# RWKV inverses as full-array products, and outputs' products with a common stationary merged

## The reference, cut to what matters

```
def step(state, inp):
    r_t, w_t, k_t, v_t, kk_t, a_t = inp
    sa = jnp.einsum('bhvk,bhk->bhv', state, -kk_t)
    state = (state * w_t[:, :, None, :]
             + sa[..., None] * (kk_t * a_t)[:, :, None, :]
             + v_t[..., None] * k_t[:, :, None, :])
    return state, jnp.einsum('bhvk,bhk->bhv', state, r_t)
```

## Time and profile before

| | us |
|---|---|
| median of 3 runs | 2262.66 |
| lowest and highest | 2260.02, 2272.73 |
| profiled execution, its own time | 2271.0 |
| its span in the trace | 2269.2 |
| inverses, 1423.8 to 1484.9 | 61.1 |
| outputs, 1485.6 to 1513.2 | 27.6 |

### The profile page before, as it was taken

One profiled execution on the slowest core, in us unless ns is written; L12 is line 12 of the kernel. 1 busy time (PEld: TensorE's weight loads), 2 busy tenths in 40 slices (PEclk: granted clock), 3 DMA queues, 4 the chain that ended last, 5 costly groups with the idle time before them and its releaser, 6 DMA issues.

```text
span 2269.2 us, 33265 instructions
## 1 busy us (share of the span) xinstructions
PE 2169.4 (96%) x14214; PEld 1782.5 (79%) x14214; DVE 1408.1 (62%) x1456; ACT 1030.6 (45%) x1155; POOL 80.5 (4%) x138
## 2 busy tenths in 40 slices
PE   6999899999999899999999999889999999999999
PEld 4777777688787777778788897777888888887887
DVE  5767744689775744499765655466556675635664
ACT  4344322467545422377644545335445444535443
POOL 2040000000000000000000000000000000020000
PEclk9998899999999899999999998999999999999999
DMA  9863879999660858999555550006555556433553
GB/s 346 329 224 110 292 252 371 366 336 367 207 241 7 275 205 307 331 344 368 186 186 188 167 182 1 4 11 215 186 186 166 195 172 204 147 95 120 195 186 112
DMA packets 267314, 475.62 MB, mean 210 GB/s; under 512 B 9424, under 2 KB 151824, under 8 KB 262944
## 3 DMA queue, kind: packets, MB, share of 16 engines
q1 hardware_dynamic: 256128, 431.81, 54.8%
q0 software_dynamic: 11040, 41.70, 5.5%
HBM read 471.33 MB, written 2.14 MB: 209 GB/s over the span
## 4 chain that ended last, share of the span: by engine, by line
PE 85%; DVE 7%; ACT 4%; DMA 3%; issue 2%; SPq 0%; ACTq 0%; DVEq 0%
PE psum L1069 14%; PE psum L1071 7%; PE psum L1086 3%; PE psum L1088 3%; PE psum L1087 3%; PE psum L1037 3%; PE psum L1038 3%; PE psum L1039 3%; PE psum L1406 3%; PE psum L1361 2%; PE psum L1362 2%; PE psum L1363 2%; PE psum L1518 2%; PE psum L1520 2%; PE psum L1519 2%; DVE w_lo L2798 2%
## 5 line engine op out<-in xcount | busy, mean ns | idle before, releaser
L2798 DVE TENSOR_TENSOR w_lo<-ring,w_hi 128x2048 fp32r<-128x2048 f32 x267 | 609.9, 2289 | 290.8 <-ACT w_hi L2149 284.8
L2149 ACT ACTIVATE w_hi<-ring 128x2048 fp32r<-128x2048 f32 x267 | 510.8, 1915 | 363.9 <-PE psum L1088 119.8
L1069 PE MATMUL psum<-h_both,w_hi 128*128 128x512 f32 x1408 | 499.7, 399 | 1.7 <-DVE h_both L3492 1.3
L1071 PE MATMUL psum<-h_both,w_lo 128*128 128x256 f32 x1408 | 395.3, 281 | 0.0
L1069 PEld LDWEIGHTS psum<-h_both,w_hi 128*128 128x128 f32 x1408 | 264.5, 188 | 68.4 <-issue 1.7
L1071 PEld LDWEIGHTS psum<-h_both,w_lo 128*128 128x128 f32 x1408 | 265.9, 189 | 1.4
L2798 DVE TENSOR_TENSOR w_lo<-pool,w_hi 128x2048 fp32r<-128x2048 f32 x70 | 160.4, 2291 | 107.5 <-ACT w_hi L2149 107.1
L2149 ACT ACTIVATE w_hi<-pool 128x2048 fp32r<-128x2048 f32 x70 | 134.1, 1916 | 163.9 <-DMA pool<-in_exp_w_up 59.2
L2171 ACT ACTIVATE pool<-psum 128x512 f32<-128x512 f32 x88 | 52.6, 598 | 261.5 <-PE psum L1071 261.5
L1037 PE MATMUL psum<-w_hi,h_both 128*128 128x512 f32 (+1 forms) x352 | 141.8, 403 | 6.6 <-DVE w_lo L2798 4.4
L1361 PE MATMUL psum<-h_both,w_hi 128*128 128x256 f32 x480 | 139.1, 290 | 0.6 <-DVE w_lo L2798 0.6
(11 more groups left out here) (476 smaller groups left out, 3813.2 us busy)
## 6 DMA issues: line engine op xcount, KB each, us to landing
ring<-in_ffn_pre_w_in SPq DMA_DIRECT2D x44, 1024.0 KB, 5.1
ring<-in_ffn_post_w_in SPq DMA_DIRECT2D x44, 1024.0 KB, 5.1
pool<-in_exp_w_up SPq DMA_DIRECT2D x40, 1024.0 KB, 7.9
ring<-in_exp_w_gate SPq DMA_DIRECT2D x36, 1024.0 KB, 7.6
ring<-in_exp_w_down SPq DMA_DIRECT2D x30, 1024.0 KB, 7.6
ring<-in_ada_w SPq DMA_DIRECT2D x24, 1024.0 KB, 7.1
ring<-in_ffn_pre_w_out SPq DMA_DIRECT2D x22, 1024.0 KB, 4.9
ring<-in_ffn_post_w_out SPq DMA_DIRECT2D x22, 1024.0 KB, 4.9
```

Of the source, the lines that this page charges most:

```text
L1069: pe.matmul(o.rearrange("p (s n) -> p s n", s=2), wh[:, k, fs], h_both[:, :, k, :], start=k == 0, stop=False, skip_group_check=True)
L1071: m = pe.matmul(o[:, 0:T], wl[:, k, fs], h_hi[:, k, :], start=False, stop=k == KD - 1, skip_group_check=True)
L2149: act.activation(w_hi[:, (s["split"] + r) % 3, :], piece(s["pieces"][r]), ACT.Copy)\
L2798: dve.tensor_tensor(w_lo[:, slot, :], piece(s["pieces"][r]), w_hi[:, slot, :].bitcast(F32), ALU.subtract).then_inc(sem("w_lo"), 1)
```

## The change

L and M are now stored as 128x128 matrices, of which the blocks that would mix two chunks hold zeros. GpSimd writes the zeros once, before the inverses (four memsets); ScalarE then copies L in four pieces for a group where it copied two, each of 64 partitions, into the other blocks, and VectorE masks M in four pieces where it had two. One product with a 128x128 stationary then serves both chunks: X = L T and M v take 4 products for each s in place of 8. In the outputs two products that share a stationary are issued as one with 128 moving columns (`both` makes an address of two strips): the inverse with kk and U, and `neg_g` with b and `out_m`. `neg_g` and `neg_h` move to columns that held L.

```diff
--- before.py
+++ after.py
@@ -354,6 +354,11 @@
         def bank(b, n=1):
             return psum[:, b, :] if n == 1 else psum[:, b:b + n, :].rearrange("p b n -> p (b n)")
 
+        def both(first, second):
+
+            return bass.AP(tensor=first.tensor, offset=first.offset,
+                           ap=[first.ap[0], [second.offset - first.offset, 2], *first.ap[1:]])
+
         def view(off, *dims):
             n = int(np.prod(dims))
             v = pool[:, off:off + n]
@@ -531,13 +536,14 @@
         gate = view(HT, NT, 768)
 
         kk_tok = xn[:, :, 0:768]
-        t_lt = [[view(PROJ + 3072 + 512 * r + 256 * s_, 4, CHUNK) for s_ in range(2)] for r in range(2)]
-        t_t = [view(PROJ + 4096 + 256 * s_, 4, CHUNK) for s_ in range(2)]
-        t_x = [view(PROJ + 4608 + 256 * s_, 4, CHUNK) for s_ in range(2)]
-        t_m = [view(PROJ + 5120 + 256 * s_, 4, CHUNK) for s_ in range(2)]
+        t_lt = [[view(PROJ + 3072 + 1024 * r + 512 * s_, 4, P) for s_ in range(2)] for r in range(2)]
+        t_t = [view(PROJ + 5120 + 256 * s_, 4, CHUNK) for s_ in range(2)]
+        t_x = [view(PROJ + 5632 + 256 * s_, 4, CHUNK) for s_ in range(2)]
+        t_m = [view(PROJ + 6144 + 512 * s_, 4, P) for s_ in range(2)]
+        t_lt_all, t_m_all = view(PROJ + 3072, 16, P), view(PROJ + 6144, 8, P)
         turn = pool[:, ROWS + 1536:ROWS + 3840].rearrange("p (w c n) -> p w c n", w=2, c=3)
-        neg_g = [view(PROJ + 5632 + 512 * r, NT, P) for r in range(2)]
-        neg_h = [view(PROJ + 5888 + 512 * r, NT, P) for r in range(2)]
+        neg_g = [view(PROJ + 3072 + 512 * r, NT, P) for r in range(2)]
+        neg_h = [view(PROJ + 3328 + 512 * r, NT, P) for r in range(2)]
         out_m = [
             pool[:, WORK + 4608 + 512 * r:WORK + 5120 + 512 * r].rearrange("p (e w t n) -> p e w t n", e=2, w=2, t=NT)
             for r in range(2)]
@@ -870,6 +876,11 @@
             pl.dma_start(view(ROWS + 3072, 1024), scratch_mem[0]).then_inc(sem("mem_in"), 16)
             pl.wait_ge(sem("norm_T"), 8 * (NORMS.index("n_mix0") + 1))
             pl.dma_start(rw_reset, a["c_reset"]).then_inc(sem("route_in"), 16)
+            pl.wait_ge(sem("rw_bonus_ps"), 1)
+            pl.memset(t_lt_all[0:64, :, 0:64], 0.0)
+            pl.memset(t_lt_all[64:P, :, 64:P], 0.0)
+            pl.memset(t_m_all[0:64, :, 64:P], 0.0)
+            pl.memset(t_m_all[64:P, :, 0:64], 0.0).then_inc(sem("rw_lt"), 1)
             pl.wait_ge(sem("x_new"), 7)
             pl.dma_start(view(ROWS + 3072, 1024), scratch_mem[1]).then_inc(sem("mem_in"), 16)
             pl.wait_ge(sem("x_new"), 8)
@@ -1782,16 +1793,13 @@
                                     m.then_inc(sem("rw_tt_ps"), 1)
                     if l < 5:
                         if l == 0:
-                            pe.wait_ge(sem("rw_lt"), 2 * g + 2)
+                            pe.wait_ge(sem("rw_lt"), 4 * g + 5)
                         for s in range(2):
                             pe.wait_ge(sem("rw_t"), 10 * g + 2 * l + s + 1)
                             for m4 in range(4):
-                                for q in range(2):
-                                    m = pe.matmul(bank(s)[halves[q], 64 * m4:64 * m4 + 64], t_lt[g % 2][s][halves[1 - q], m4, :],
-                                                  t_t[s][halves[1 - q], m4, :], start=True, stop=True)
-                                    m_last[q] = m
-                            for m in m_last:
-                                m.then_inc(sem("rw_x_ps"), 1)
+                                m = pe.matmul(bank(s)[:, 64 * m4:64 * m4 + 64], t_lt[g % 2][s][:, m4, :], t_t[s][:, m4, :],
+                                              start=True, stop=True)
+                            m.then_inc(sem("rw_x_ps"), 2)
                     if l == 0:
                         chunk_products(g, (6, 7), Fk, W[3])
                         for m in m_last:
@@ -1801,13 +1809,9 @@
                         for s in range(2):
                             i = 2 * g + s
                             for m4 in range(4):
-                                for hq in halves:
-                                    v = v_tok[hq, m4 % 2, P * i + 64 * (m4 // 2):P * i + 64 * (m4 // 2) + 64]
-                                    m = pe.matmul(bank(6 + s)[hq, 64 * m4:64 * m4 + 64], t_m[s][hq, m4, :], v,
-                                                  start=True, stop=True)
-                                    m_last[hq.start // 64] = m
-                            for m in m_last:
-                                m.then_inc(sem("rw_u_ps"), 1)
+                                v = v_tok[:, m4 % 2, P * i + 64 * (m4 // 2):P * i + 64 * (m4 // 2) + 64]
+                                m = pe.matmul(bank(6 + s)[:, 64 * m4:64 * m4 + 64], t_m[s][:, m4, :], v, start=True, stop=True)
+                            m.then_inc(sem("rw_u_ps"), 2)
                     if l == 4 and g < 2:
                         pe.wait_ge(sem("rw_u"), 2 * g + 2)
                         later(g + 1)
@@ -1843,11 +1847,10 @@
                         pe.wait_ge(sem("rw_gh"), 1)
                     for m4 in range(4):
                         t, o = m4 % 2, 128 * i + 64 * (m4 // 2)
-                        for w, right in enumerate((kk_tok, U)):
-                            for hq in halves:
-                                m = pe.matmul(bank(3)[hq, P * m4 + 64 * w:P * m4 + 64 * w + 64], TT[hq, i, m4, :],
-                                              right[hq, t, o:o + 64], start=True, stop=True)
-                                m_last[hq.start // 64] = m
+                        for hq in halves:
+                            m = pe.matmul(bank(3)[hq, P * m4:P * m4 + P].rearrange("p (w n) -> p w n", w=2), TT[hq, i, m4, :],
+                                          both(kk_tok[hq, t, o:o + 64], U[hq, t, o:o + 64]), start=True, stop=True)
+                            m_last[hq.start // 64] = m
                     for m in m_last:
                         m.then_inc(sem("rw_gh_ps"), 1)
                 if i >= 1:
@@ -1860,14 +1863,18 @@
                     begun -= {(6, 0), (6, 1), (7, 0), (7, 1)}
                     quarters = [(e, q) for e in range(2) for q in range(2)]
                     for t in range(NT):
-                        for e, q in quarters:
-                            m_last[q] = pe.matmul(bank(6 + q)[halves[e], 256 + 64 * t:320 + 64 * t], neg_g[r][halves[q], t, halves[e]],
-                                                  out_m[r][halves[q], e, 0, t, :], start=first(6 + q, e), stop=True,
-                                                  skip_group_check=True)
                         ahead = [(e, q, slice(P * j + 64 * e, P * j + 64 * e + 64)) for e, q in quarters if 2 * t + q < 3]
                         for e, q, cols in ahead:
-                            pe.matmul(bank(6 + q)[halves[e], 64 * t:64 * t + 64], neg_g[r][halves[q], t, halves[e]],
-                                      b_tok[halves[q], t, cols], start=False, stop=True, skip_group_check=True)
+                            m_last[q] = pe.matmul(both(bank(6 + q)[halves[e], 64 * t:64 * t + 64],
+                                                       bank(6 + q)[halves[e], 256 + 64 * t:320 + 64 * t]),
+                                                  neg_g[r][halves[q], t, halves[e]],
+                                                  both(b_tok[halves[q], t, cols], out_m[r][halves[q], e, 0, t, :]),
+                                                  start=first(6 + q, e), stop=True, skip_group_check=True)
+                        if t == 1:
+                            for e in range(2):
+                                m_last[1] = pe.matmul(bank(7)[halves[e], 320:384], neg_g[r][halves[1], t, halves[e]],
+                                                      out_m[r][halves[1], e, 0, t, :], start=False, stop=True,
+                                                      skip_group_check=True)
                         for e, q, cols in ahead:
                             pe.matmul(bank(6 + q)[halves[e], P + 64 * t:P + 64 * t + 64], b_tok[halves[q], t, cols],
                                       neg_h[r][halves[q], t, halves[e]], start=False, stop=False, skip_group_check=True)
@@ -2490,8 +2497,10 @@
 
                 act.wait_ge(sem("rw_l_ps"), 4 * g + 2)
                 for s in range(2):
-                    act.activation(t_lt[g % 2][s].rearrange("p (e t) n -> p e (t n)", e=2),
-                                   psum[:, 6:8, P * s:P * s + P], ACT.Copy).then_inc(sem("rw_lt"), 1)
+                    dst = t_lt[g % 2][s].rearrange("p (e t) n -> p e t n", e=2)
+                    src = psum[:, 6:8, P * s:P * s + P].rearrange("p e (t n) -> p e t n", t=NT)
+                    for q in range(2):
+                        act.activation(dst[halves[1 - q], :, :, halves[q]], src[halves[1 - q]], ACT.Copy).then_inc(sem("rw_lt"), 1)
 
             later(0)
             for g in range(3):
@@ -3410,10 +3419,13 @@
             def tiles(v):
```

(11 more changed lines are left out.)

## The result

The changed kernel takes 2272.98 us (median of 19 runs, 2267.36 to 2279.52), the kernel before 2261.69 (19 runs beside it, 2256.85 to 2272.73). The ratio is 1.0048, with a 95% interval of 1.0039 to 1.0057. That is 10.9 us slower (8.8 to 12.9), where the predicted 2272.0 stood for +9.3 us. All ratios here leave out one run that was much slower at a mean granted clock of 0.65 (3103.26 us, of the kernel with M v on quarters).

A forecast was written before the change was run, and what follows sets the result against it. Two close limits on TensorE: instruction supply in 16 KB blocks, at best one in 3.8 us, and the products' time. 17.6 - 5.9 - 2.4 - 0 = +9.3 us on 2262.7 gives 2272.0; eight in ten from 2256 to 2282.

The forecast's parts named there:

- X and M v, +17.6: Inverses: half as many full-array records, each nearly four times as costly; 5.9 us a group, three groups +17.6.
- The full drain: Changes between full array and quarters: draining TensorE, 0.22 us at 30 changes, would add 3 us to the sum.
- What was costed at nothing: VectorE's four masks of M, ScalarE's two more copies of L and POOL's memsets: all hidden, 0 us.
- The refund, -5.9: Inverses: 288 fewer records end all seven instruction pauses, 4.7 us of idle and 0.16 each hidden.
- Outputs, -2.4: Outputs: merged products -0.3, pauses before 1499 gone -1.9, a last bit near 1511 -0.2.
- The third pause: Outputs, L1848 at 1501.6: removing its 0.6 us gives nothing, as TensorE then waits for VectorE's mask.
- half the clock behind the longer wait: Outputs: the wait for VectorE might cool the clock and cost more than now (0.94 granted); a sign of being wrong.
- The free full array: Rival: X's full-array records run at 0.058, as fast as quarter pairs; 2254 to 2256 us; chance 0.13.
- the refund that does not come: Rival: pauses not due to the instruction count, so the 8 us stay; +17.3, 2280 us; chance 0.15.
- the hidden X: Rival: VectorE's and ScalarE's round trip sets the levels, X grows beside it; 2257 to 2259 us; chance 0.10.

The follow-up runs named there:

- The shifted streams: Kernel before with 32, then 16, small products put ahead of the chunk products; inverses 59.57 us and 60.99 us.
- the added waits: Four long-met waits after each m4 of X: in the kernel before ratio 1.0057, inverses 71.92 us; in the changed kernel 1.0065, 73.83 us.
- the run with half of X: Kernel before with only m4 = 0 and 1 of the X products, the other half left out; inverses 54.72 us.
- the run with the split moved: Kernel before with merged outputs, one weight split moved from round 3 to 5 on ScalarE and behind the rounds on VectorE; ratio 0.9982, outputs 21.31 us.
- Outputs alone: Kernel before with only the outputs' products merged, L and M left in quarters; ratio 0.9991, outputs 23.43 us.

## Why the prediction was right

The change measured +10.9 us (8.8 to 12.9) for the forecast of +9.3. That the time itself, 2272.98, lies within 1 us of 2272.0 is luck in part, since the kernel before took 1 us less beside it than the 2262.66 the forecast started from. Two of the sums are 0.1 to 0.2 off: three groups of 5.9 are 17.7, and 4.7 and seven times 0.16 are 5.8, so the whole comes to +9.5 with its own terms.

**X and M v, +17.6: right.** The table above gives 5.9 a group. The 0.16 for the first and 0.112 for the other records came out at 1.72 us for 15 of them, 0.115; X to T at a plain level at 1.93 for the 1.90 taken; level 2 at 3.72 for 3.7. Inside the group parts were off and cancel: level 0 cost 1.00 in place of 1.4, level 4 cost 1.17 in place of 0.8, and 0.31 of level 1's 0.93 are VectorE's masks, which the prediction had at nothing. Without them X and M v are 5.6 a group, 16.9 in all, and the masks 0.9; that the two together hit 17.6 is luck. The change back to quarters, 0.07 before the end of the last full record in the earlier trace rows, was 0.07 here too (1.72 + 0.275 - 1.93), and the comparison with M v on quarters gives it as 0.09 a change. The full drain of the Trainium skill (TensorEngine Tiling, section Key Properties), which was weighed at +3 us, isn't seen: T starts 0.07 us before the modelled end of the last full record.

**What was costed at nothing.** One of these was mis-sized: VectorE's masks of M. I had four instructions at 0.33. On 64 partitions they start 0.43 apart (1.74 for four), where those on 128 partitions start 0.33 apart. So they end 1.74 after X's start in place of 1.4, and hold T back by 0.31 a group, 0.9 in all; the run with the masks moved gives 0.87 of it back. ScalarE's copies and POOL's memsets were hidden as said; the memsets took 3.0 us of the 4 assumed.

**The refund, -5.9: right in sum and in kind.** All seven pauses went. The loss of 17.8 by the table, less the inverses' measured +11.7, leaves 6.1 for it. The shifted streams and the added waits show that the pauses lie 256 instructions apart by count. What the prediction said too loosely is that blocks can be summed over the stretch (14.6 blocks, 56 us), at 3.8 us each: the run with half of X shows that what 256 instructions in a row take is what counts, and a block that has to wait took 3.5 to 4.1 us. For the changed kernel both readings give the same.

**Outputs, -2.4: right, the parts too.** 24.88 us where 25 was forecast. The third pause gave nothing, as said: the wait for VectorE grew from 1.9 to 2.8 as TensorE came earlier, and the run with the split moved shows that 2.1 us (23.43 to 21.31) were under it. The profile of the changed kernel has half the clock behind the longer wait, which the prediction named as a danger. Outputs alone took 23.43 with the same products at the full clock, so this was 1.4 us of the 24.88. The profile of the kernel before has the same 3.4 us at half the clock, so it cancels in the -2.4. That both had it is luck: with the fall in one of them alone the difference would have read -1.0 or -3.9.

**The rivals.** The free full array (0.058 a pair) is excluded by the 0.115; the refund that does not come by the missing pauses; the hidden X by the table, where every level grew. For the last the run with half of X shows how near it was from the other side: with X shorter TensorE does wait for the others.

## What to carry to other kernels

A 128x128 stationary matrix with two zero blocks is not one product for two. In float32 its record costs 0.112 us here, by all signs the load of 128 columns, whether 64 or 128 columns are moved, while two quarter products run side by side at 0.058 for the pair. Merging products that have the same stationary matrix takes records away and made nothing longer here (behind the wait in the outputs 5.79 us merged and 5.83 unmerged, both at the full clock). Where TensorE's idle time is "issue", find what 256 of its instructions in a row take (127 matmuls with their loads) before counting on a gain: in the kernel before the blocks with a pause held 2.7 to 3.0 us of work, and in all runs 68 of 70 such blocks held 3.6 us or less. Then look which engine's wait stands next behind the pause.

## What the runs showed that I had not expected

- A group of four waits that are long met costs 0.09 to 0.15 us between quarter products and 0.009 between full-array ones.
- A VectorE operation on 64 partitions by 256 elements starts every 0.43 us, one on 128 by 256 every 0.33: half the partitions were not cheaper, and which part the new layout of the output has in it was not tried.
- While POOL ran its memsets, four small copies of VectorE (L3412) took 0.60 us in place of 0.39 in the kernel before. That the memsets are the cause was not tried, and the inverses did not start later (1423.2 us, before 1423.8).
